# Gate and up products of a feed-forward layer in two matmuls instead of three, with their halves added afterwards

## What is computed

```
D_MODEL = 1024; SEQ = 256
D_FF = ((8 * D_MODEL // 3 + 255) // 256) * 256     # 2816
CONV_WIDTH = 3
# per layer: y = rms_norm(x) * norm_ffn
#   gate = y @ w_gate            (256 tokens x 2816)
#   up   = y @ w_up              (256 tokens x 2816)
#   gate = causal depthwise conv over tokens, 3 taps, plus bias
#   x    = x + (gelu(gate) * up) @ w_down
```

## Time and profile before

| | |
|---|---|
| median of 3 runs | 1074.33 us (1074.14 to 1074.9) |
| time of the profiled execution | 1075.35 us |
| its span, first to last instruction | 1072.7 us |
| PE busy, share of the span | 1064.1 us, 99% |
| PEld busy | 949.9 us, 89% |
| DVE busy | 721.6 us, 67% |
| ACT busy | 574.9 us, 54% |
| POOL busy | 141.2 us, 13% |
| HBM traffic over the span | 154 GB/s |
| mean granted clock of TensorE | 0.999 of full speed |

### The profile page before, as it was taken

The page is one execution under the profiler, slowest core; times in us unless marked ns, Lnnn a source line. Parts: engine busy times, 40 slices in busy tenths (PEclk is TensorE's granted clock), DMA queues, the critical chain, the costliest instruction groups (busy, mean ns, idle before and its releaser), DMA issues.

```text
span 1072.7 us, 19921 instructions
## 1 busy us (share of the span) xinstructions
PE 1064.1 (99%) x8092; PEld 949.9 (89%) x8092; DVE 721.6 (67%) x1230; ACT 574.9 (54%) x977; POOL 141.2 (13%) x166
## 2 busy tenths in 40 slices
PE   9999999999999999999999999999999999999998
PEld 7887878656898999799999999999998799999997
DVE  5665566387554878778875676666677776766674
ACT  4532676544444567866565554444574555545454
POOL 0000010253200001632531000000023410000000
PEclk9999999999999999999999999999999999999999
DMA  9732121286613442057444364555543334555641
GB/s 382 319 137 66 75 79 40 93 289 213 232 41 119 141 145 80 6 193 236 148 168 158 119 236 161 194 186 170 198 155 103 134 119 153 202 201 177 211 178 39
DMA packets 25386, 168.77 MB, mean 157 GB/s; under 512 B 3280, under 2 KB 3536, under 8 KB 5456
## 3 DMA queue, kind: packets, MB, share of 16 engines
q1 hardware_dynamic: 25152, 167.25, 44.1%
q10 hardware_dynamic: 144, 0.26, 0.1%
HBM read 164.35 MB, written 1.05 MB: 154 GB/s over the span
## 4 chain that ended last, share of the span: by engine, by line
PE 96%; DVE 2%; ACT 2%; issue 0%; DVEq 0%; ACTq 0%
PE bank L437 26%; PE bank L438 25%; PE bank L439 25%; PE bank L1550 2%; PE bank L494 2%; PE bank L1714 2%; PE bank L1704 2%; PE bank L1694 1%; PE bank L1577 1%; PE bank L1568 1%; PE bank L446 1%; PE bank L2363 1%; PE bank L1395 1%; DVE wlo L415 1%; ACT TILE L1753 1%; PE bank L1688 1%
## 5 line engine op out<-in xcount | busy, mean ns | idle before, releaser
L437 PE MATMUL bank<-OPH,whi 128*128 128x256 f32 (+1 forms) x1716 | 519.7, 303 | 0.3
L439 PE MATMUL bank<-OPH,wlo 128*128 128x256 f32 (+1 forms) x1716 | 511.2, 298 | 0.0
L438 PE MATMUL bank<-OPL,whi 128*128 128x256 f32 (+1 forms) x1716 | 511.2, 298 | 0.0
L415 DVE TENSOR_TENSOR wlo<-raw,whi 128x1024 fp32r<-128x1024 f32 (+1 forms) x255 | 304.0, 1234 | 101.4 <-ACT whi L400 101.3
L437 PEld LDWEIGHTS bank<-OPH,whi 128*128 128x128 f32 x1716 | 328.0, 191 | 17.3 <-issue 5.2
L438 PEld LDWEIGHTS bank<-OPL,whi 128*128 128x128 f32 x1716 | 328.2, 191 | 10.0 <-issue 1.2
L439 PEld LDWEIGHTS bank<-OPH,wlo 128*128 128x128 f32 x1716 | 328.0, 191 | 9.8
L400 ACT ACTIVATE whi<-raw 128x1024 fp32r<-128x1024 f32 (+1 forms) x255 | 254.9, 1050 | 74.2 <-PE bank L439 71.9
L437 PE MATMUL bank<-whi,OPH 128*128 128x256 f32 (+2 forms) x272 | 93.8, 345 | 0.2 <-DVE OPL L717 0.2
L438 PE MATMUL bank<-wlo,OPH 128*128 128x256 f32 (+2 forms) x272 | 91.1, 335 | 0.0
L439 PE MATMUL bank<-whi,OPL 128*128 128x256 f32 (+2 forms) x272 | 91.1, 335 | 0.0
(11 more groups left out here) (291 smaller groups left out, 1132.6 us busy)
## 6 DMA issues: line engine op xcount, KB each, us to landing
raw<-in_stream SPq DMA_DIRECT2D x143, 1024.0 KB, 4.9
PROJ<-in_stream SPq DMA_DIRECT2D x5, 1024.0 KB, 18.4
raw<-in_stream SPq DMA_DIRECT2D x4, 1056.0 KB, 8.6
PROJ<-PROJ SPq DMA_DIRECT2D x32, 64.0 KB, 3.9
FIRST<-in_first SPq DMA_DIRECT2D x1, 1248.0 KB, 5.9
C<-in_con SPq DMA_DIRECT2D x1, 1157.5 KB, 7.2
FIRST<-in_first SPq DMA_DIRECT2D x1, 1024.0 KB, 8.0
WST<-in_w_s SPq DMA_DIRECT2D x2, 256.0 KB, 7.3
```

The lines of the kernel that those rows point to most:

```text
L415: nc.vector.tensor_tensor(c.w[1][:, part], c.raw[:, part], c.w[0][:, part].bitcast(F32), ALU.subtract).then_inc(*raises(c.lo[h]))
L437: nc.tensor.matmul(out, w[0], x[0], start=start, stop=False, skip_group_check=skip)
L438: nc.tensor.matmul(out, w[0], x[1], start=False, stop=False, skip_group_check=skip)
L439: return nc.tensor.matmul(out, w[1], x[0], start=False, stop=stop, skip_group_check=skip)
```

## The change

The operand's high and low part are laid side by side for each k in one tensor `OPS`. A gate or an up is then made with two matmuls for each (k, t): one of 512 columns, in which the high weights meet high and low operand at once and whose result is a whole bank (hi*hi in columns 0 to 255, hi*lo in columns 256 to 511), and one of 256 columns, low weights by high operand, added onto the first half. Each gate and each up thus takes two banks (gates 2 and 3, ups 0 and 1, each time the same). Afterwards ACT copies the second halves of both banks to SBUF (`copy_halves`), and DVE adds the first halves to them (`add_halves`); only then comes the multiplication by `rr`, now from SBUF.

In each engine's program some instructions are placed otherwise. "Third chunk" in the change's name is the chunk of gate1, and its `split_hi` is written out ahead of the first `copy_halves`. The `split_hi` of up1 comes behind the norm's factor instead of ahead of it. The `split_hi` of `by["up", c].s + 4` comes ahead of the copy that makes the hidden values' high part. The splits at the end of ffn0 are cut in halves and laid between the additions to x.

```diff
-        OPH, OPL = sb("OPH", [P, KD, T], F32R), sb("OPL", [P, KD, T], F32R)
+        OPS = sb("OPS", [P, KD, 2, T], F32R)
+        OPH, OPL = OPS[:, :, 0, :], OPS[:, :, 1, :]
...
+        def products_apart(bank, w, k, lo, start, stop):
+            both = bank[:].rearrange("p (a b) -> p a b", b=SEQ)
+            nc.tensor.matmul(both, w[0], OPS[:, k, :, lo:lo + SEQ], start=start, stop=False, skip_group_check=True)
+            return nc.tensor.matmul(bank[:, 0:SEQ], w[1], OPH[:, k, lo:lo + SEQ], start=False, stop=stop,
+                                    skip_group_check=True)
...
+            g_both, up_both = twin[1], twin[0]
             for c in range(NF):
-                g.append(GBANK.take("pe", ("dve",)))
-                up.append(GBANK.take("pe", ("dve",)))
+                g.append([b.take("pe", ("dve",)) for b in banks[2:4]])
+                up.append([b.take("pe", ("dve",)) for b in banks[0:2]])
...
-            def wide(e, u, ch):
-                for point in due(e, u.empty, ch.lo):
+            def wide(e, us, ch):
+                for point in due(e, ch.lo):
                     e.wait_ge(*point)
-                for t in range(2):
+                for t, u in enumerate(us):
+                    for point in due(e, u.empty):
+                        e.wait_ge(*point)
                     for k in range(KD):
-                        mm = products(u.mem[:, t * SEQ:(t + 1) * SEQ], cols(ch, k, t * P, P), op(k, lo, SEQ), k == 0,
-                                      k == KD - 1)
-                mm.then_inc(*raises(u.full))
+                        mm = products_apart(u.mem, cols(ch, k, t * P, P), k, lo, k == 0, k == KD - 1)
+                    mm.then_inc(*raises(u.full))
+
+            def copy_halves(e, what, c, us, both):
+                for point in due(e, us[0].full, us[1].full, ("halves_summed", l, c - 1, what) if c else None):
+                    e.wait_ge(*point)
+                nc.scalar.activation(part[what], both[:, :, SEQ:2 * SEQ], ACT.Copy).then_inc(
+                    *raises(("low_copied", l, c, what)))
+
+            def add_halves(e, what, c, out, both):
+                for point in due(e, ("low_copied", l, c, what)):
+                    e.wait_ge(*point)
+                nc.vector.tensor_tensor(out, both[:, :, 0:SEQ], part[what], ALU.add).then_inc(
+                    *raises(("halves_summed", l, c, what)))
...
             def act(e):
                 operand.act(e)
                 log_exp_table()
+                split_hi(e, first.s + 3)
+                copy_halves(e, "gate", 0, g[0], g_both)
+                inverse_root(e, f"ffn{l}", r, total.tot.mem[:, 0:SEQ], 1.0 / D, total.full, total.tot.read["act"])
                 split_hi(e, first.s + 4)
-                inverse_root(e, f"ffn{l}", r, total.tot.mem[:, 0:SEQ], 1.0 / D, total.full, total.tot.read["act"])
                 for c in range(NF):
                     split_hi(e, by["gate", c].s + (3 if c else 4))
+                    if c:
+                        copy_halves(e, "gate", c, g[c], g_both)
...
                     nc.scalar.activation(t1[c].mem[:], t1[c].mem[:], ACT.Gelu).then_inc(*raises(("gelu_made", l, c)))
+                    copy_halves(e, "up", c, up[c], up_both)
+                    split_hi(e, by["up", c].s + 4)
...
                     nc.scalar.activation(HH[c % 2], two(t2[c].mem), ACT.Copy).then_inc(*raises(("h_hi_made", l, c)))
-                    split_hi(e, by["up", c].s + 4)
...
             def dve(e):
-                    split_lo(e, by["gate", c].s + (3 if c else 4))
+                    padded = pad[c % 2][:, :, 2:SEQ + 2]
+                    if c:
+                        split_lo(e, by["gate", c].s + 3)
...
-                    nc.vector.tensor_tensor(pad[c % 2][:, :, 2:SEQ + 2], two(g[c].mem), rr, ALU.mult).then_inc(*raises(("gate_scaled", l, c)))
+                    add_halves(e, "gate", c, padded, g_both)
+                    if c == 0:
+                        split_lo(e, first.s + 4)
+                    nc.vector.tensor_tensor(padded, padded, rr, ALU.mult).then_inc(*raises(("gate_scaled", l, c)))
...
-                    nc.vector.tensor_tensor(two(t2[c].mem), two(up[c].mem), rr, ALU.mult).then_inc(*raises(up[c].read["dve"]))
+                    add_halves(e, "up", c, two(t2[c].mem), up_both)
+                    nc.vector.tensor_tensor(two(t2[c].mem), two(t2[c].mem), rr, ALU.mult).then_inc(*tick("dve"))
...
-                g[c].freed[:] = [("gate_scaled", l, c)]
+                for i in range(2):
+                    g[c][i].freed[:] = [("halves_summed", l, c, "gate")]
+                    up[c][i].freed[:] = [("halves_summed", l, c, "up")]
```

More of the change, by code:

```diff
@@ L2968, in dve @@
                             if tap:
-                                ins.then_inc(*raises(("older_tap", l, c, b)))
+                                ins.then_inc(*raises(("conv_done", l, c, "older", b)))
                             else:
-                                ins.then_inc(*raises(("conv_done", l, c) if b else ("conv_half_done", l, c)))
+                                ins.then_inc(*raises(("conv_done", l, c) if b else ("conv_done", l, c, "half")))
                         if tap:
-                            e.wait_ge(*when(("older_tap", l, c, 1)))
+                            e.wait_ge(*when(("conv_done", l, c, "older", 1)))
                     split_lo(e, by["up", c].s + 3)
-                    for point in due(e, up[c].full, t2[c].empty):
+                    for point in due(e, t2[c].empty):
                         e.wait_ge(*point)
-                    nc.vector.tensor_tensor(two(t2[c].mem), two(up[c].mem), rr, ALU.mult).then_inc(*raises(up[c].read["dve"]))
-                    for point in due(e, ("gelu_made", l, c), up[c].read["dve"]):
+                    add_halves(e, "up", c, two(t2[c].mem), up_both)
+                    for point in due(e, ("halves_summed", l, c, "up")):
+                        e.wait_ge(*point)
+                    nc.vector.tensor_tensor(two(t2[c].mem), two(t2[c].mem), rr, ALU.mult).then_inc(*tick("dve"))
+                    e.wait_ge(*ticked("dve"))
+                    for point in due(e, ("gelu_made", l, c)):
                         e.wait_ge(*point)
@@ L2986, in dve @@
                     split_lo(e, by["up", c].s + 4)
-                split_lo(e, by["down", NF - 1].s + 3)
                 for i, a in enumerate(acc if l == 0 else ()):
@@ L3005, in ffn @@
             s.used = [("down_added", l, NF - 1)]
-            s.operand_used = [up[NF - 1].full]
+            s.operand_used = [up[NF - 1][1].full]
             return s
```

39 lines of the change are left out of this document (24 added, 15 removed).

## The result

| | before | changed |
|---|---|---|
| median | 1074.49 us (1074.14 to 1074.9, 4 runs) | **1082.57 us** (1081.86 to 1083.46, 4 runs) |
| profiled execution | 1075.35 us | 1082.05 us |
| its span | 1072.7 us | 1080.2 us |
| mean granted clock | 0.999 | 0.996 |

The changed kernel takes 1.0074 times as long (interval 1.0059 to 1.0089): 8.1 us slower, where 1.9 us were forecast, and outside the range.

A forecast was written before the change was run, and what follows sets the result against it. PE was taken to bound the kernel, busy 99% of the span. Waits less the 4.69 us saving gave +1.07 us in ffn0 and +0.82 in ffn1, +1.9 together: 1076.2 us, range 1074.4 to 1079.8.

The forecast's parts named there:

- The saving: Gates and ups of both layers: each (k, t) falls from 0.360 to 0.3467 us, 4.69 us a layer, 9.39 in all.
- Rival 1: At up1's wait: the clock falls while PE waits; one fall gives 1077.5 to 1078 us, two 1079 to 1080; chance 0.3.
- The start of each layer: First gates and ups, where nothing covers copies and additions: waits net of down0's gain sum to 5.76 us in ffn0.
- up0's bank: Layer start: up0 waits for bank 1, still read by DVE's last addition of the projection; 0.4 us with PE's restart.
- gate1: Layer start: gate1 waits for gate0's banks until copy and addition are done; cost 0.76 us.
- up1: Layer start: up1 waits for up0's banks, whose addition stands behind the convolution; 4.2 us, 4.25 with the restart.
- down0's wait: Before down0 in ffn0: the earlier wait of 0.3 to 0.4 us for its split goes, -0.4 us.
- The waits of gate2 and up2 in ffn0: gate2 and up2 of ffn0 wait because DVE's low parts end later; 0.5 and 0.25 us.
- Rival 2: Gate and up pairs: overhead hangs on something besides matmul count, such as bank or weights' reading; 1083.8 us, chance 0.04.
- Rivals 3 and 4: Mid-layer waits of 0.2 us per c, 1079.4 us, chance 0.06; shorter start-up than the walk, 1067.4 us, chance 0.06.
- the hole at up1: PE's one gap in the first 30 us of each layer, ahead of up1, about 4.2 us.
- three signs: Prediction wrong if the pair isn't 0.347 us, up1's hole is under 3.5 or over 5 us, or the clock falls there.

The follow-up runs named there:

- e_filled: Changed kernel with 14 filler matmuls of 128 columns written on PE between gate1 and up1 of both layers; 1079.99 us, ratio 1.0046.
- e_widths: Changed kernel plus loops of 32 matmul pairs of various widths behind its last matmul, one execution; 512 + 256 columns, each its own bank, 0.353 us.

## Why the prediction was wrong

**The saving** is the step that failed: "between zero (the overhead stays per 256 columns) and 9.39 us I take 9.39, since both distances hold right up to the change from one kind to the other". The rows had the two widths one behind the other once, not in turn. In turn the pair takes 0.3533 us, not 0.3467; the overhead of a pair is 0.0333 us instead of the 0.0267 of two matmuls, against 0.04 of the three before. 704 x (0.360 - 0.3533) = 4.7 us; five chunks at the faster pace (gate0 and up0 of both layers, gate1 of ffn0) give 80 x 0.0067 = 0.5 more. So the saving is 5.2 us, 4.2 less than priced. The mechanism, fewer matmuls and less overhead, was right; its size was about half. This alone nearly carries the time out of the range: with the clock kept up (e_filled) it was still 1079.99 us, against an upper bound of 1079.8. Why the two widths in turn cost more than alone is open.

**Rival 1**, the clock, came true in both layers, at about 1.5 us each against 1.8 priced (1.3 net, by e_filled). It had a chance of 0.3; I took "only 0.6 us longer than what was still endured" as evidence against it, but that 3.5 us had ended in a fall. It speaks for one.

**The start of each layer** was right to some tenths. up0's bank cost 0.37 us (0.4 forecast), gate1 0.76 (as forecast, restarts counted before and after), up1 3.91 and 3.82 with 0.08 more for its restart (4.25 forecast with it); down0's wait went. The waits of gate2 and up2 in ffn0 (0.75) didn't come, since PE arrived later at the slow clock, as rival 1 had it; in e_filled, at full clock, about 0.4 us of them did. Together 4.8 us in ffn0 (5.76 forecast) and 5.1 in ffn1 (5.51).

**Not foreseen:** the down products of ffn1 took 5.50 us instead of 5.47, 0.3 us over eleven. They run among pairs now; why they are slower was not tried.

**The account.** Forecast 1.9, saving short by 4.2, clock 3.0, waits less by 1.4, downs 0.3: 8.0 us. In the profiled executions PE's last matmul ended 7.4 us later although ffn0 began 0.3 us earlier, so the stretch from ffn0 on took 7.8 us more. The medians differ by 8.1; the profiled execution was one of the two shorter of four. The two longer ones had a mean clock of 0.994 and 0.995 instead of 0.996, which would fit a fall of 6.8 us instead of 3.4, but they have no trace.

**Rivals 2 to 4.** Rival 2 came true in part: a pair saved 0.0067 us instead of 0.0133, so the overhead does hang on more than the count of matmuls, to which I gave a chance of 0.04. It is not the bank, which that rival named: with a bank for each width the pair took 0.353 us as well (e_widths). Rivals 3 and 4 did not happen: mid-layer has no wait, and the start-up was not shorter.

**What the trace was to show:** 0.2267 and 0.120 us by turns with 11.09 us between gate and down was wrong (11.31); the two waits for `halves_summed` and the hole at up1 were right; the hole was inside its bounds of 3.5 to 5 us. Of the three signs that the prediction had named as proof against itself, two appeared: the pair did not take 0.347 us, and the clock fell in the hole.
